# Tile 8's third score chunk and its exponentials moved ahead of the third V projection in the A units

## What the reference computes

```
s = einsum('bqhd,bshd->bhqs', q, k) * DH_A ** -0.5
p = softmax(where(mask, s + cq - ck, -inf))       # FoX: cumulative log-forget as a bias
o = einsum('bhqs,bshd->bqhd', p, v)
```

## Time and profile before

| | us |
|---|---|
| median of 3 runs | 1928.03 (1927.21 to 1929.28) |
| the profiled execution: its time | 1927.87 |
| the profiled execution: its span | 1926.3 |

### The profile page before, as it was taken

The page is one execution under the profiler, slowest core; times in us unless marked ns, Lnnn a source line. Parts: engine busy times, 40 slices in busy tenths (PEclk is TensorE's granted clock), DMA queues, the critical chain, the costliest instruction groups (busy, mean ns, idle before and its releaser), DMA issues.

```text
span 1926.3 us, 32815 instructions
## 1 busy us (share of the span) xinstructions
PE 1787.0 (93%) x12006; PEld 1313.2 (68%) x12006; DVE 1143.6 (59%) x2340; ACT 776.9 (40%) x1329; POOL 109.2 (6%) x183
## 2 busy tenths in 40 slices
PE   6779999999999999996899989999999999999997
PEld 4436666666655555554899976668976679766697
DVE  4745565646576767667654378775247762477621
ACT  3535555555555556565312234442013330133311
POOL 3020100001010101000000000000000000000011
PEclk9889999999999999998899999999999999999999
DMA  7050514333141405043343211111111111111121
GB/s 257 12 150 2 152 52 99 104 86 118 35 126 27 133 13 146 7 120 115 114 136 102 80 44 44 46 52 44 44 44 44 54 39 49 44 44 54 41 85 46
DMA packets 153836, 144.77 MB, mean 75 GB/s; under 512 B 7880, under 2 KB 133938, under 8 KB 153760
## 3 DMA queue, kind: packets, MB, share of 16 engines
q1 hardware_dynamic: 135168, 78.29, 15.2%
q0 software_dynamic: 18592, 65.46, 10.5%
HBM read 112.61 MB, written 31.11 MB: 75 GB/s over the span
## 4 chain that ended last, share of the span: by engine, by line
PE 76%; DVE 9%; issue 5%; ACT 5%; DMA 4%; POOL 1%; DVEq 0%; ACTq 0%; SPq 0%; POOLq 0%
PE bank L761 41%; PE psS L761 18%; PE psO L761 11%; PE psT L971 2%; DMA gate<-gate_scr 2%; DMA cum_s<-c_scr 2%; DVE peak_w L1573 1%; DVE sc L1814 1%; PE psT L761 1%; PE bank L831 1%; ACT pT_h L1157 1%; ACT sc L1347 1%; DVE m_a L1912 0%; DMA x_tm<-in_x_prompt 0%; PE psT L795 0%
## 5 line engine op out<-in xcount | busy, mean ns | idle before, releaser
L761 PE MATMUL bank<-xn_hi,w_h 128*128 128x364 f16 (+1 forms) x952 | 304.9, 320 | 22.7 <-DVE xn_lo L1560 15.1
L761 PE MATMUL bank<-xn_lo,w_h 128*128 128x364 f16 (+1 forms) x952 | 304.2, 319 | 0.0
L761 PE MATMUL bank<-xn_hi,w_l 128*128 128x364 f16 (+1 forms) x952 | 303.7, 319 | 0.0
L761 PE MATMUL psS<-x_h,wf_l 128*128 128x364 f16 (+1 forms) x528 | 167.7, 318 | 0.0
L761 PE MATMUL psS<-x_h,wf_h 128*128 128x364 f16 (+1 forms) x528 | 167.7, 318 | 0.0
L761 PE MATMUL psS<-x_l,wf_h 128*128 128x364 f16 (+1 forms) x528 | 167.7, 318 | 0.0
L1478 ACT ACTIVATE ct<-u,vecs 128x1090 f32<-128x1090 f32 x44 | 57.1, 1297 | 258.9 <-DVE u L2029 233.4
L761 PEld LDWEIGHTS bank<-xn_hi,w_h 128*128 128x128 f16 x952 | 93.6, 98 | 84.4 <-issue 24.7
L761 PEld LDWEIGHTS bank<-xn_hi,w_l 128*128 128x128 f16 x952 | 93.8, 99 | 54.5 <-issue 1.1
L1560 DVE SCALAR_TENSOR_TENSOR pT_l<-psT,pT_h 128x1024 f16<-128x1024 f32 (+8 forms) x72 | 54.4, 756 | 122.6 <-ACT pT_h L1157 122.6
L761 PEld LDWEIGHTS bank<-xn_lo,w_h 128*128 128x128 f16 x952 | 93.8, 99 | 47.5 <-issue 0.9
(11 more groups left out here) (379 smaller groups left out, 4259.9 us busy)
## 6 DMA issues: line engine op xcount, KB each, us to landing
wraw<-in_w_up SPq DMA_DIRECT2D x44, 512.0 KB, 3.8
wraw<-in_w_in SPq DMA_DIRECT2D x41, 512.0 KB, 7.5
gate<-gate_scr POOLq DMA_DIRECT2D x16, 544.0 KB, 4.6
wraw<-in_w_down SPq DMA_DIRECT2D x16, 448.0 KB, 3.4
x_scr<-xT POOLq DMA_DIRECT2D x8, 544.0 KB, 6.0
cum_s<-c_scr POOLq DMA_DIRECT2D x8, 544.0 KB, 7.7
sqq<-rt_scr SPq DMA_DIRECT2D x16, 272.0 KB, 4.0
sqk<-rt_scr SPq DMA_DIRECT2D x16, 272.0 KB, 5.6
```

The lines of the kernel that those rows point to most:

```text
L761: return pe.matmul(out, w, x, start=first, stop=last, **kw)
```

## The change

For the one tile with three score chunks (`split_tail`, n = 2), A units now take the branch that B units had. The list becomes S(8,1), T(5,0), AV(6,1), VC, S(8,2), E(8), VCL, V2, T(5,1), S(4,0), and goes on as before. So S(8,2) moves ahead of V2 and VCL, and E(8) ahead of V2's evacuation and of T(5,1). B units are as they were. No instruction is added or removed.

```diff
-        if split_tail and kind == "B":
+        if split_tail:
             act_flush()
             scores(n + 1, 2)
             plan.append(("E", TILES[n + 1]))
         flush()
         jobs((n, 0))
-        if split_tail and kind == "A":
-            scores(n + 1, 2)
         if kind == "A":
             plan.append(("T", i, 1))
-        if split_tail and kind == "A":
-            plan.append(("E", TILES[n + 1]))
```

## The result

The changed kernel takes 1938.23 us (median of 5 runs, 1936.57 to 1940.74), the kernel before 1928.05 us; the ratio is 1.0047, with a 95% interval of 1.0034 to 1.0060, so 6.6 to 11.6 us slower. The forecast was slower by 6.4 us. The point, 1934.4, was 3.8 us too low, and the median lies 0.4 us above the range's upper end; by the ratio, on the 1928.03 us from which the forecast started, the time is 1937.1 us, inside the range.

The account below looks back on a forecast made before the run. The prediction took an A unit to be as long as PE's work plus its few waits. A PE wait for DVE at S(8,2), 6.4 us over four units, added to 1928.03 gave 1934.4 us, range 1931.4 to 1937.8.

Parts of the forecast that it names:

- PE arrives at 274.88 and waits for DVE: At S(8,2) in A units: PE waits until 276.50 for DVE's first map of S(8,1), 6.4 us over four units.
- The boundaries between kinds of work at nothing: On PE: as many boundaries as before, so no cost, within 0.2 us each way over four units.
- E(8) is hidden under V2, with 0.45 us to spare: On ACT: both exponentials run under V2; may be 0.45 us late at no cost; 0.8 us allowed at the upper end.
- The gain allowed at the lower end: At PE's 0.34 us wait ahead of S(4,1): likeliest gain nothing, at most the whole wait, 1.4 us.
- DVE in the old order has slack under V2: Between S(8,1) and S(8,2) in the old order: V2's 3.76 us on PE hide DVE's lateness.
- The loss is carried through the start of the next unit: At A unit starts: the DMA awaited there moves with PE, so nothing counted back; rival of loss taken back, chance 0.09.
- The clock: Behind the new hole: rival that the clock falls, 1.7 us each, 1936.1 for one fall to 1941.2 for four; chance 0.15.
- The prediction's own sign of being wrong: In the stretches around the holes: a clock below 1.00, one of three listed signs that the forecast is wrong.
- The rival's own figure for two falls: Whole kernel, if the clock falls behind two of the new holes: 1937.8 us; chance 0.15 for one or more falls.

Follow-up runs that it names:

- r3: Changed kernel, but E(8) stays behind T(5,1) in A units, so only S(8,2) moves: 1940.40 us, 1.0054 of the kernel before.
- r5: Changed kernel, but in A units DVE makes the low half of the K weights behind VCL: 1930.59 us, 1.0004 of the kernel before.
- r7: Changed kernel plus one useless DVE reduction (1.22 us) ahead of S(8,1) in A units: 1946.37 us, 1.0093 of the kernel before.
- r6: Kernel before, but in A units only E(8) moves, ahead of T(5,1), with S(8,2) still behind V2: 1946.56 us, ratio 1.0092.
- r4: Changed kernel, but in A units PE issues 12 of V2's 24 matmuls ahead of S(8,2): 1938.19 us, 1.0046 of the kernel before.
- r8: Kernel before plus one useless DVE reduction ahead of S(8,1) in A units, old order kept: 1930.62 us, ratio 1.0008.
- r1: Changed kernel run again, unaltered: 1939.16 us, 1.0052 of the kernel before.
- r11: Changed kernel run once more, unaltered: 1939.51 us, 1.0055 of the kernel before.

## Why the prediction was right, and where it was too small

*PE arrives at 274.88 and waits for DVE:* right. The wait is there in all four units, ended by DVE's minimum, with the 0.06 us of the earlier trace rows. r3 shows that S(8,2)'s move alone makes the loss, r5 that it goes when DVE's lateness goes, r7 that more lateness adds to it. Predicted 6.4 us; measured 5.9. The profile prints the hole as 1.45 instead of 1.62 us, since it counts idle time only from the modelled end of the last AV matmul.

*The boundaries between kinds of work at nothing:* a small miss, and it is the 0.5 us between 6.4 and 5.9. From S(8,2) to T(5,1) PE's work was put at 4.45 us and takes 4.37; from T(5,1) to S(4,1) it took 3.43 us before and takes 285.61 - 282.23 = 3.38 now. Together that gives back 0.13 us a unit, 0.5 us over four; the bound was 0.2. The other units of the three profiles show the same two figures, wherever no fall of the clock lies between.

*E(8) is hidden under V2, with 0.45 us to spare:* hidden it is, but with less to spare: E(8) ends at 282.13 + 0.19 = 282.32, 0.11 us ahead of V2's evacuation where 0.21 was worked out, since its two exponentials take 2.48 us from their start instead of 2.37; behind the evacuation 0.10 us is left (283.09 - 282.99) instead of 0.24. r6 and r4 show the price as soon as the cover is short: 2.1 and 1.1 us a unit. The gain allowed at the lower end (the 0.34 us ahead of S(4,1)) didn't come: 0.32 us stay.

*DVE in the old order has slack under V2:* right. r8's added work costs 1.3 us over four units by the medians, 1.7 by the means, less than the 2.5 expected there.

*The loss is carried through the start of the next unit:* right. PE's waits at the start of the second, third and fourth A unit in the changed kernel:

```profile
244.54 0.50 PE L757 MATMUL psS<-k_h,q_h 64*128 64x512 f32 x2 [0.92 <-DVE smin L1810]
...
351.39 0.50 PE L757 MATMUL psS<-k_h,q_h 64*128 64x512 f32 x2 [1.39 <-DVE smin L1810]
...
460.11 0.50 PE L757 MATMUL psS<-k_h,q_h 64*128 64x512 f32 x2 [1.78 <-DVE smin L1810]
```

Before they were 1.03, 0.99 and 1.61 us. In sum they are 0.46 us longer, in r1 0.29 and in r11 0.06: they vary by tenths of a microsecond, and nothing of the 5.9 us is taken back.

*The clock:* this is the step that failed. I gave its fall behind the new hole 0.15, as a rival beside the forecast, and argued from one wait of 1.61 us at 453.51 that a hole of this length doesn't bring it about. In the profiles of the changed kernel the clock falls behind 6 of 12 holes, and 3.5 us of the 9.4 are its. One row was a draw of one. The trace of before held its answer: PE idle for 1.60 us at 647.83 is followed by a fall, and the wait at the start of the fourth A unit, which I took as the evidence against, is followed by one in the changed kernel's own profile (1.78 us, above).

```profile
647.83 0.52 PE L883 MATMUL bank<-ident,o_tm 128*128 128x128 f32 x3 [1.60 <-DVE o_tm L1886]
```

```profile
645.00:655.00 10.00, 7.95 (x45) 4.89 (x43) 5.44 (x8) 6.48 (x10) 1.86 (x3) 0.83 0.20 77
```

```profile
455.00:465.00 10.00, 8.22 (x44) 4.66 (x43) 7.00 (x13) 1.53 (x3) 2.88 (x4) 0.83 0.86 324
```

The first two fences are of before, the third of the changed kernel. The prediction's own sign of being wrong, a clock under 1.00 in these stretches, came true in two of the four units. The rule that I cited beside it, from the Trainium skill's "TensorE: Matmul & The Clock Gate", section "A second HAM failure mode: psum-queue depth-cycling", agrees with these runs in part: short idle times between groups of matmuls do bring the clock down, but behind 1.4 us of idle time in half of the units only, not in each; a fall costs 1.7 us here. With 4 x 0.5 falls the sum would have been 6.4 + 3.4 = 9.8, 1937.8. The rival's own figure for two falls was that, and it stood right at the upper end of the range. With the boundaries' 0.5 us taken off, the two parts that the profiles show are 5.9 + 3.4 = 9.3 us.

What stays open: why the clock falls behind one hole and not behind another with the same instructions around it.

## What to carry to other kernels

An independent job between two dependent ones is cover for a third engine. Before such a job is moved behind both, subtract the time at which PE would arrive from the time at which the slow engine is done. The difference, here 1.6 us, is the loss. And an item moved ahead on another engine (E(8)) needs its own cover counted. It paid to look at what made DVE late: moving 1.28 us of weight work behind the critical item, in the B units, and putting half a projection into the wait ahead of S(4,1), gave 8 us where the reordering of the A units lost 9.

When PE gets a new hole of more than a microsecond, price a fall of its clock behind it as likely, in proportion to what several such waits in the trace show, and not as a rival by one of them.

## What the runs showed of the hardware

Whether the clock falls behind a hole varies between units with the same instructions. Counting the profiles at hand: none of 4 behind the 0.25 us holes (r5), 8 of 16 behind 1.4 us (6 of 12 in the changed kernel, 2 of 4 in r3), 1 of 4 behind the 1.4 us waits of r4, none of 8 when PE was kept busy with useless matmuls in that time, 8 of 8 behind 2.4 us (r6, r7). One fall costs 0.17 x 10 us = 1.7 us where PE sets the pace, as much as the hole ahead of it (1.6 us between the start that PE could have made and the one it made), and 1.1 us at the start of the fourth A unit. So work of no use in a hole was cheaper than idleness, by 2.7 and 4.7 us in two comparisons.
